# A chunk's triangular inverse by repeated squaring: results of levels two to five written across the partition halves

## What is computed

```python
def _rwkv7_scan(r, w, k, v, a_vec, b_vec, s0):
    def step(s, inp):
        rt, wt, kt, vt, at, bt = inp
        sa = jnp.einsum('bhvk,bhk->bhv', s, at)
        s = s * wt[:, :, None, :] + sa[..., None] * bt[:, :, None, :] + vt[..., None] * kt[:, :, None, :]
        y = jnp.einsum('bhvk,bhk->bhv', s, rt)
        return s, y
```

## Time and profile before

| | |
|---|---|
| median of three runs | 1575.6 us (1575.22 to 1577.18) |
| the profiled execution | 1577.94 us |
| its span | 1576.2 us |
| mean granted TensorE clock | 0.996 |
| busy: TensorE, its weight loads, VectorE, ScalarE, GpSimd | 1544.2, 1504.5, 1174.3, 775.3, 492.8 us |
| chunk loop of the first layer | from 204.0 to 331.4 us |
| chunk loop of the second layer | from 976 to 1103 us |

### The profile page before, as it was taken

The page is one execution under the profiler, slowest core; times in us unless marked ns, Lnnn a source line. Parts: engine busy times, 40 slices in busy tenths (PEclk is TensorE's granted clock), DMA queues, the critical chain, the costliest instruction groups (busy, mean ns, idle before and its releaser), DMA issues.

```text
span 1576.2 us, 41384 instructions
## 1 busy us (share of the span) xinstructions
PE 1544.2 (98%) x17631; PEld 1504.5 (95%) x17631; DVE 1174.3 (75%) x2011; ACT 775.3 (49%) x1390; POOL 492.8 (31%) x378
## 2 busy tenths in 40 slices
PE   8999999999999999999999999999999999999997
PEld 7999998989999999999999999988999999999997
DVE  4589645677768988898647894567776699898974
ACT  5455355655434445444444634556553344454445
POOL 5345432213422222222234354122233222222211
PEclk9999999999999999999999999999999999999998
DMA  5222210003332332332232222000223333323312
GB/s 152 76 68 81 81 43 5 4 13 91 94 94 85 96 88 81 97 96 77 69 100 68 81 78 78 11 4 4 59 71 101 87 94 95 94 81 95 95 54 89
DMA packets 219896, 115.45 MB, mean 73 GB/s; under 512 B 10356, under 2 KB 217474, under 8 KB 219714
## 3 DMA queue, kind: packets, MB, share of 16 engines
q1 hardware_dynamic: 219634, 112.79, 25.2%
q10 hardware_dynamic: 80, 0.02, 0.0%
HBM read 109.27 MB, written 3.53 MB: 72 GB/s over the span
## 4 chain that ended last, share of the span: by engine, by line
PE 94%; DVE 2%; issue 1%; DMA 1%; ACT 0%; POOL 0%; SPq 0%; DVEq 0%; ACTq 0%
PE ps L784 26%; PE ps L785 26%; PE ps L1363 7%; PE ps L1364 7%; PE ps L1365 7%; PE ps L1034 2%; PE ps L1037 2%; PE ps L1031 2%; PE ps L996 1%; PE ps L1008 1%; PE ps L1099 1%; DMA raw<-in_ffn_w_up 1%; PE ps L789 1%; PE ps L1306 1%; PE ps L928 1%
## 5 line engine op out<-in xcount | busy, mean ns | idle before, releaser
L665 POOL TENSOR_TENSOR wlo<-raw,whi 128x1024 fp32r<-128x1024 f32 (+1 forms) x105 | 254.6, 2425 | 411.2 <-ACT whi L1475 411.2
L760 POOL TENSOR_TENSOR wlo<-raw,whi 128x512 fp32r<-128x512 f32 x96 | 138.3, 1441 | 416.0 <-ACT whi L1956 416.0
L1475 ACT ACTIVATE whi<-raw 128x1024 fp32r<-128x1024 f32 (+1 forms) x106 | 105.4, 994 | 274.3 <-PE ps L785 266.2
L784 PE MATMUL ps<-xh,whi 128*128 128x288 f32 x608 | 181.7, 299 | 2.3 <-DVE xl L2103 1.8
L785 PE MATMUL ps<-xh,whi 128*128 128x288 f32 x608 | 179.3, 295 | 0.0
L784 PE MATMUL ps<-xl,whi 128*128 128x288 f32 x608 | 179.1, 295 | 0.0
L784 PE MATMUL ps<-xh,wlo 128*128 128x288 f32 x608 | 179.0, 294 | 0.0
L785 PE MATMUL ps<-xh,wlo 128*128 128x288 f32 x608 | 178.9, 294 | 0.0
L785 PE MATMUL ps<-xl,whi 128*128 128x288 f32 x608 | 178.8, 294 | 0.0
L784 PEld LDWEIGHTS ps<-xh,whi 128*128 128x128 f32 x608 | 114.4, 188 | 4.5 <-issue 3.1
L785 PEld LDWEIGHTS ps<-xh,whi 128*128 128x128 f32 x608 | 114.5, 188 | 0.2
(11 more groups left out here) (381 smaller groups left out, 5085.4 us busy)
## 6 DMA issues: line engine op xcount, KB each, us to landing
raw<-in_ffn_w_up SPq DMA_DIRECT2D x88, 512.0 KB, 3.9
raw<-in_w_in SPq DMA_DIRECT2D x52, 512.0 KB, 3.8
Ei<-in_ffn_w_down SPq DMA_DIRECT2D x64, 256.0 KB, 3.3
raw<-in_w_out SPq DMA_DIRECT2D x16, 512.0 KB, 4.0
raw<-in_ffn_w_down SPq DMA_DIRECT2D x16, 256.0 KB, 2.8
xin<-in_x_prompt SPq DMA_DIRECT2D x4, 512.0 KB, 6.9
Ei<-in_ffn_w_down SPq DMA_DIRECT2D x16, 128.0 KB, 3.4
out<-xin SPq DMA_DIRECT2D x8, 256.0 KB, 2.9
```

What stands on the lines that cost most here:

```text
L665: e.tensor_tensor(wlo[s][:, 0:width], raw[s][:, 0:width], whi[s][:, 0:width].bitcast(F32), ALU.subtract).then_inc(w_lo[s], 1)
L760: lo = e.tensor_tensor(by_tile(D_lo[name]), A[name], by_tile(D_hi[name]).bitcast(F32), ALU.subtract)
L784: e.matmul(acc(out)[:, 0], lhsT, rhs[:, 0:HT], start=start, stop=stop)
L1475: e.activation(whi[s][:, 0:width], raw[s][:, 0:width], ACT.Copy).then_inc(w_hi[s], 1)
```

## The change

From level two on, head X of each half writes its results to the partition half given by X and not to the one it reads: the four products of an operation (two partition halves, two X) use four quarters of the array. The partition half that is read picks the bank. Half A writes in both banks of `gr` (PSUM tile 0), half B in both banks of `tk` (tile 1). Since partition half and X change places at each level, so do the heads; level five's result is put back in order as it is copied.

The sum is made otherwise. The running product is multiplied by (power + identity). `next_factor`, on VectorE, adds the identity to the copied power and writes a new tile `factor`, for which it waits for ScalarE's copy. The old running product no longer needs an add; the new one is copied back by ScalarE together with the powers, three slots instead of two (at level four two instead of one). Level five's results of both halves are copied to `Tf` in one instruction, `keep_inverse`. In VectorE's order `next_factor` for level two stands between `add_rest` and `mask_scores`.

```diff
-DV_F = ["D", "E", "MA", "MB", "L2A", "L2B", "L3A", "L3B", "L4A", "L4B", "L5A", "L5B"]
+DV_F = ["D", "E", "MA", "MB", "L1A", "L1B", "L2A", "L2B", "L3A", "L3B", "L4A", "L4B", "L5A", "L5B"]
...
+        factor = w2a2[:, 4 * C:8 * C].rearrange("p (h x t) -> p h x t", h=2, x=2)
...
                 def level(j, hp, k):
 
-                    N, d = "AB"[hp], DET[(k + 1) % 2]
-                    powers = gr[hp][:, 0:4 * C].rearrange("p (x c t) -> p x c t", x=2, c=2)
-                    product = pair3(tk[hp][:, 0:2 * C])
+                    N, d, banks = "AB"[hp], DET[(k + 1) % 2], (gr, tk)[hp]
                     if k == 1:
+                        powers = gr[hp][:, 0:4 * C].rearrange("p (x c t) -> p x c t", x=2, c=2)
                         front(dv_f, DV_F, j, "M" + N)
-                    else:
+                        for X in range(2):
+                            for h in HEADS:
+                                e.matmul(powers[h, X, 0], d[h, hp, X, 2], d[h, hp, X, 0], start=True, stop=True)
+                            for h in HEADS:
+                                mm = e.matmul(powers[h, X, 1], d[h, hp, X, 0], d[h, hp, X, 2], start=True, stop=True)
+                        mm.then_inc(pe_f, 1)
+                        return
+                    if k == 2:
+                        front(ac_f, AC_F, j, "L1B")
+                    elif k < 5:
                         front(ac_f, AC_F, j, f"L{k - 1}{N}")
-                        if k == 2:
-                            front(po_f, PO_F, j, "T" + N)
-                            front(ac_f, AC_F, j, "tok")
-                        else:
-                            front(dv_f, DV_F, j, f"L{k - 1}{N}")
-                    for X in range(2):
-                        for h in HEADS:
-                            if k < 4:
-                                mm = e.matmul(powers[h, X, 0], d[h, hp, X, 2], d[h, hp, X, 0], start=True, stop=True)
-                        for h in HEADS:
-                            if k < 5:
-                                mm = e.matmul(powers[h, X, 1], d[h, hp, X, 0], d[h, hp, X, 2], start=True, stop=True)
-                        for h in HEADS:
-                            if k > 1:
-                                mm = e.matmul(product[h, X], d[h, hp, X, 2], d[h, hp, X, 1], start=True, stop=True)
+                    else:
+                        front(ac_f, AC_F, j, "L4B")
+                    if k < 4:
+                        for i, h in enumerate(HEADS):
+                            for X in range(2):
+                                e.matmul(banks[i][HEADS[X], 0:C], d[h, hp, X, 2], d[h, hp, X, 0], start=True, stop=True)
+                    if k < 5:
+                        for i, h in enumerate(HEADS):
+                            for X in range(2):
+                                e.matmul(banks[i][HEADS[X], 2 * C:3 * C], d[h, hp, X, 0], d[h, hp, X, 2], start=True, stop=True)
+                    if k == 2:
+                        front(po_f, PO_F, j, "T" + N)
+                    front(dv_f, DV_F, j, f"L{k - 1}{N}")
+                    for i, h in enumerate(HEADS):
+                        for X in range(2):
+                            out = banks[i][HEADS[X], C:2 * C] if k < 5 else tk[i][HEADS[X], hp * C:(hp + 1) * C]
+                            mm = e.matmul(out, factor[h, hp, X], d[h, hp, X, 1], start=True, stop=True)
                     mm.then_inc(pe_f, 1)
...
                 def copy_powers(j, hp, k):
 
                     step(pe_f, PE_F, j, f"L{k}" + "AB"[hp])
-                    src = gr[hp][:, 0:4 * C].rearrange("p (x c t) -> p x c t", x=2, c=2)
-                    if k < 4:
-                        e.activation(DET[k % 2][:, hp, :, 0:3:2, :], src, ACT.Copy).then_inc(ac_f, 1)
-                    else:
-                        e.activation(DET[k % 2][:, hp, :, 2, :], src[:, :, 1, :], ACT.Copy).then_inc(ac_f, 1)
+                    if k == 1:
+                        src = gr[hp][:, 0:4 * C].rearrange("p (x c t) -> p x c t", x=2, c=2)
+                        e.activation(DET[1][:, hp, :, 0:3:2, :], src, ACT.Copy).then_inc(ac_f, 1)
+                    else:
+                        kept_slots = slice(0, 3) if k < 4 else slice(1, 3)
+                        src = PS[hp].rearrange("p (x c t) -> p x c t", x=2, c=8)[:, :, kept_slots, :]
+                        e.activation(DET[k % 2][:, hp, :, kept_slots, :], src, ACT.Copy).then_inc(ac_f, 1)
...
-                def add_power(j, X, k):
-
-                    N = "AB"[X]
-                    step(pe_f, PE_F, j, f"L{k}{N}")
-                    if k == 2:
-                        step(po_f, PO_F, j, "T" + N)
-                    else:
-                        step(dv_f, DV_F, j, f"L{k - 1}{N}")
-                    src = pair3(tk[X][:, 0:2 * C])
-                    dst = DET[k % 2][:, X, :, 1, :] if k < 5 else Tf[j % 2][:, 2 * X:2 * X + 2, :]
-                    e.tensor_tensor(dst, DET[(k + 1) % 2][:, X, :, 1, :], src, ALU.add).then_inc(dv_f, 1)
+                def next_factor(j, X, k):
+
+                    step(ac_f, AC_F, j, f"L{k}" + "AB"[X])
+                    e.tensor_tensor(factor[:, X], DET[k % 2][:, X, :, 2, :], ident2[:, :].unsqueeze(1).broadcast_to([P, 2, C]),
+                                    ALU.add).then_inc(dv_f, 1)
+
+                def keep_inverse(j):
+
+                    step(pe_f, PE_F, j, "L5B")
+                    e.tensor_copy(Tf[j % 2].rearrange("p (h x) t -> p x h t", h=2),
+                                  PS[1].rearrange("p (x c t) -> p x c t", x=2, c=8)[:, :, 0:2, :]).then_inc(dv_f, 2)
...
                     if i >= 0:
                         add_rest(i)
+                    next_factor(j, 0, 1)
+                    next_factor(j, 1, 1)
                     mask_scores(j)
...
                     for k in (2, 3, 4):
-                        add_power(j, 0, k)
-                        add_power(j, 1, k)
+                        next_factor(j, 0, k)
+                        next_factor(j, 1, k)
...
                     new_gla_state(j)
-                    add_power(j, 0, 5)
-                    add_power(j, 1, 5)
+                    keep_inverse(j)
```

More of the change, by code:

```diff
@@ L1014, in level @@
                 def level(j, hp, k):
-                    N, d = "AB"[hp], DET[(k + 1) % 2]
-                    powers = gr[hp][:, 0:4 * C].rearrange("p (x c t) -> p x c t", x=2, c=2)
-                    product = pair3(tk[hp][:, 0:2 * C])
+                    N, d, banks = "AB"[hp], DET[(k + 1) % 2], (gr, tk)[hp]
                     if k == 1:
+                        powers = gr[hp][:, 0:4 * C].rearrange("p (x c t) -> p x c t", x=2, c=2)
                         front(dv_f, DV_F, j, "M" + N)
-                    else:
-                        front(ac_f, AC_F, j, f"L{k - 1}{N}")
-                        if k == 2:
-                            front(po_f, PO_F, j, "T" + N)
-                            front(ac_f, AC_F, j, "tok")
-                        else:
-                            front(dv_f, DV_F, j, f"L{k - 1}{N}")
@@ new lines, in level @@
+                        mm.then_inc(pe_f, 1)
[3 more added lines that the diff above has]
+                    elif k < 5:
+                        front(ac_f, AC_F, j, f"L{k - 1}{N}")
+                    else:
+                        front(ac_f, AC_F, j, "L4B")
[3 more added lines that the diff above has]
+                                e.matmul(banks[i][HEADS[X], 0:C], d[h, hp, X, 2], d[h, hp, X, 0], start=True, stop=True)
```

## The result

The changed kernel takes **1590.7 us** (median of 4 runs, 1589.8 to 1591.6), the kernel before 1576.4 beside it: 1.0091 [1.0079, 1.0102] of the time, 14.3 us slower. (In the four executions of the kernel before beside it one of 3366.7 us is counted in the median; the 55 later ones, in three groups, have medians of 1576.2 to 1576.9.) The forecast was 1574.1 with a range of 1563 to 1583, so the result lies outside, on the slow side. The profiled execution of the changed kernel took 1589.8 us, its span 1588.0, 11.8 more than before.

A forecast was written before the change was run, and what follows sets the result against it. Copies and VectorE, not TensorE alone, end last once products shrink: of 37.8 us array time saved, gains and losses sum to -0.75 us a layer, -1.5 for both, giving 1574.1 us against the 1575.6 median; range 1563 to 1583.

The forecast's parts named there:

- The ordinary pass up to the gla products: Pass j = 6: output sum moves from 4.78 to 4.3 us, gla products from 5.45 to 5.00.
- rival 4: Inverse levels: the four quarters don't overlap, only waits are added, 7.5 us a layer, 1591; chance 0.05.
- rival 3: VectorE's queue between `add_rest` and `centre`: head-of-line waits make it slower, 6.6 us in all, 1582; chance 0.20.
- The level-four factors in ordinary passes: At j = 6, factors due at 6.46 wait behind GpSimd until 7.30; 0 instead of -0.6 us; j = 4 at -0.2.
- The rule on the lock: VectorE instructions with two SBUF inputs contend with GpSimd reading SBUF; whichever started first holds the other; j = 6 at 0.
- The last pass: j = 8: `centre` loses the 1.2 us head start, L737 and L739 meet the factors, level five ends 0.8 late.
- H: Head of line: `next_factor` ahead of `centre` in VectorE's order; at j = 7 `centre` ends at 3.07 instead of 1.61.
- G: Factors with two SBUF inputs wait while a GpSimd product runs; at j = 6 this takes the 0.6 us gain.
- The first three passes: Passes j = 0, 1 and 2, without `centre`: gains of 0.8, 0.85 and 1.1 us.
- level two's 0.70 us: At j = 1, level two stands behind a statistics product anyway, so its 0.70 is saved whole; pass -0.85.
- The clock: Both chunk loops, 127.4 and 127.0 us long, were taken at full granted clock.
- 0.6, 0.8 and 0.8: Losses in us forecast for passes j = 5, j = 7 (both with two statistics) and j = 8 (the last).

The follow-up runs named there:

- e7: Changed kernel with the three GpSimd products of the loop cut to one column of each group: 1584.7 us, 1.0052 of the kernel before.
- e8: Kernel before the change with the three GpSimd products of the loop cut to one column of each group: 1574.8 us, 0.9992.
- e1: Changed kernel with level two's `next_factor` moved behind `mask_scores` and `centre` on VectorE: 1577.3 us, 1.0007 of the kernel before.
- e11: Changed kernel with e1's move and e7's short GpSimd products together: 1573.4 us, 0.9979 of the kernel before.
- e9: Kernel before with levels two and three crossed, power and product merged, identity added on TensorE: 1573.2 us, 0.998.
- e10: e9 with only the crossing undone, so levels two and three use two quarters: 1585.4 us, 1.0054 of the kernel before.
- e4: Changed kernel without `next_factor`; an identity product on TensorE after each product makes the sum, 64 more records a pass: 1598.4 us, 1.0142.
- e5: e4 with next power and product merged into one 128-column instruction, 32 fewer records a pass: 1584.8 us, 1.006 of the kernel before.
- e3: Kernel before without the power products of levels two and three, 64 fewer records a pass, no wait added: 1560.8 us, 0.9896.

## Why the prediction was wrong

**Right, in place and size.** `centre` 1.4 us later at j = 7 (1.44), L804 behind it, level two at +1.44; L5 of j = 5 and j = 7 in the first layer +0.62 and +0.75 against +0.6 and +0.8 (in the second, +2.63 and +0.71). The ordinary pass up to the gla products: output sum 4.31 (4.3), gla products 4.98 (5.00). The four quarters do overlap; rival 4's 1591 is met in number only. The way in which it was slower is rival 3, in its place, at twice its price (6.6 forecast, 14.3 measured).

**Wrong, by step:**

- *The level-four factors in ordinary passes* (2.0 us too little). The forecast had `scale_o` end near 5.9 and GpSimd at 7.30, so that the pass "gains nothing". But VectorE's order has the level-three factors ahead of `scale_o`, and they wait for the level-three copies (0.41 us in the row at 296.28). `scale_o` ends at 6.47 and L731 at 7.91. L5: +0.51 at j = 6 (0 forecast), +1.08 at j = 4 (-0.2 forecast). The rule on the lock was right, and e7 and e8 measure it; the head-of-line wait was seen at `centre` and overlooked one level further down in the same queue. On the lock the Trainium skill ("SBUF — State Buffer", section "Who interferes with whom": a VectorE instruction with two SBUF inputs contends with a GpSimd instruction that reads SBUF) and the trace agree: 1.57 beside L731 in after, 0.60 in e7.
- *The last pass.* 0.8 forecast, 2.19 and 2.18 measured; 0.49 and 0.74 in e1, -0.36 and -0.27 in e7. `centre` 1.22 late was right; the output sum then is 1.33 late (7.14 against 5.81), and behind it copy and factor of level four stand in line, 0.85 more, where the forecast counted L737 and L739 only. The forecast had both H and G here and put them together at 0.8.
- *The first three passes.* -2.75 a layer forecast; -1.01 and +1.00 measured. This was the term that carried the forecast's gain, and it is the largest miss, 5.5 us in both layers. It took level two's 0.70 us as saved whole at j = 1, and read the earlier trace rows as slack that the saving fills. But the stalls without releaser were supply: they don't shrink with the products, they grow.
- *The supply, missing altogether.* The forecast priced a record at 14.6 ns from runs of 14 and 16 records, far fewer than the 128 of a packet. It let none of the 144 records a pass pay for arrival. Supply stalls rise from 14.3 to 24.4 us.
- *The clock.* The earlier trace rows at 1.00 was taken to hold after. By the estimate above it costs 3 us, and the second layer has the larger misses (j = 3 and 5 at +1.67 and +2.63, where 1.5 and 1.9 us of supply stall come just ahead of the two stretches above).

**The account of the 14.3 us.** Order of `next_factor` with the clock that goes with it 13.4 (e1); GpSimd beyond what it costs before 2.3 (e11 to e1, 3.9, less e8's 1.6); all the rest of the change -1.4 (e11 to e8). It closes by construction; each term is a difference of medians with some 2 us of its own uncertainty, so the last two can't be told from nothing in size. From the forecast's -1.5 to the measured 14.3 are 15.8 us. The forecast has no price of H by itself: its 0.6, 0.8 and 0.8 are net of what the levels give back. But the passes show where it went wrong: of the 13.3 us of the table, 7.5 lie in passes without `centre`, where H has no part, and 5.9 in those with it. So the mechanism that the forecast feared was real and dearer than it thought, and the gain that it set against it wasn't there. That -1.4 is so near the forecast's -1.5 is luck.

**Left open.** How the 5.5 us of the first three passes divide between supply and other waits was not taken apart. A factor read from PSUM might avoid G, as the adds in the earlier trace rows do, but then VectorE and ScalarE would read the same bank; it was not tried. What sets the 3.22 us between packets isn't seen in these traces.

## What to carry to other kernels

When a step is given a new producer in a queue written by hand, follow that queue from the new wait to the end of the pass: every step behind it pays, at each level where the pattern repeats, and moving the step behind what it has nothing to do with cost nothing here. Before counting array time saved as time saved, take from the trace how often instruction packets land and how many records come in each; of products that run faster than that rate only a part of the saving comes through (12.2 of 33 us in e9 against e10), and making them fewer (one wide product instead of two with the same stationary operand) was worth more here: 13.6 us from e4 to e5. And a saving in a loop with hidden waits should be discounted by an experiment such as e3, which leaves products out with no wait added: here one half was left.

## What the runs showed of the hardware

- TensorE's instructions come in packets of 16 KB, 128 matmul records with their weight loads, which take about 1 us and never start less than 3.22 us apart in the loops. A stall for them ends 1.2 to 1.6 us after the packet's end and reads as "issue", often in the middle of a line's records.
- Small float32 64x64 products: 29 ns a record in two quarters, 15 in four. The shortest distance of two packets gives 25 ns a record as an estimate of the best that the supply allows over a longer run.
- Two 128x128 operations of VectorE with both inputs in SBUF took 0.56 to 0.68 us alone and 1.57 beside a GpSimd product of 1.29; the same sum read from PSUM had stayed at 0.29 each.
- The four stretches at half the full clock in the changed kernel's loops follow 4 us in which TensorE was busy 0.9 to 2.5 us; over all runs 0.001 of mean granted clock goes with 1.16 us of this kernel.
